# Start of a two-layer encoder trunk: products on the first 512 features, separate buffers for four w_ada blocks, another load order, and the rotary additions before the first maximum

## The chip, the cores and the metric

The kernel runs on one core of one Trainium2 chip. The metric is device time in microseconds (us) of one execution. The kernel before takes 1368.41 us, median of 3 runs (1368.14 to 1368.48).

## The reference

Two layers over 512 tokens of 1024 features, float32. In each layer (cut to what matters here):

```
c_act = silu(c)
mod = c_act @ w_ada[l] + b_ada[l]                 # 1024 -> 6144, six vectors of 1024
sh_a, sc_a, g_a, sh_m, sc_m, g_m = split(mod, 6)
h = x * (1 + sc_a) + sh_a
proj = h @ w_in[l]                                # 1024 -> 2208: a_q a_k a_v | b_cq b_ckv b_kr | c_q c_k c_v
y_a = dilated_mixture(a_q, a_k, a_v, rel_bias)    # 4 heads, bias per head from t5_bucket(key - query)
y_b = mla_attention(b_cq, b_ckv, b_kr, ...)       # 4 heads, 32 rotary features of 96
y_c = axial_gqa(c_q, c_k, c_v, ...)               # 8 query heads, 2 key heads
x = layer_norm(ALPHA * x + (1 + g_a) * (concat(y_a, y_b, y_c) @ w_o[l]))
h = x * (1 + sc_m) + sh_m
x = layer_norm(ALPHA * x + (1 + g_m) * (square(relu(h @ w1[l])) @ w2[l]))
```

## The kernel before

Each engine has its instructions written out in program order, and semaphores tie them together. Every float32 product is made of three fp32r products (`three`: high x high, high x low, low x high), so each weight slab (128 rows of a weight matrix, up to 512 columns) is loaded to `slab_raw`, copied to `slab_hi` by ScalarE (ACT) and subtracted to `slab_lo` by VectorE (DVE). These two are called the split of a slab. A ring of eight slab buffers is refilled by SyncE's queue (SP) in program order: slab i is issued only when slab i - 8 has been used, and all that stands behind it in the queue waits with it.

The first layer's start, which the change is about, goes so:

- `ada_load`, `ada_piece`: the vectors `mod` are made in blocks of 512 columns. A block of `w_ada` (2 MB) comes in two halves of 512 rows (1 MB each) into the two buffers `ada_w`; DVE adds up eight pieces per block (scalar times 128x512, plus the sum so far) in `ada_sum`, and TensorE (PE) adds over the partitions with a column of ones (`mod_cols`). A half may be loaded when the half two before it has been used. Blocks 0 and 1 are the shift `sh_a`, 2 and 3 the scale `sc_a`. All four are made first (`AHEAD = 4`).
- Between the blocks DVE and PE make one head's row of relative bias (`relb`, `onehot`, `lncnt`, `frow`: 128 equal rows of 1024), and ACT stores all of it in DRAM as `bias_rows` (2 MB). It is read back with a skew into `bands` during attention.
- Then x is transposed (`transpose_x`, tokens 0 to 255 as job `lnp`, 256 to 511 as `lnq`), scaled and shifted by ACT (`ln_evac`) and split in high and low (`hT_hi`, `hT_lo`, DVE: `ht_low`).
- `first_chunk` and `chunk_job` multiply it chunk by chunk with `w_in`: `cqa` (slabs 0 to 7), `cqkv` (8 to 15), `bcq` (16 to 23), `bckv` (24 to 31), `av` (32 to 39), then the transposes `tc` and `tk`, then `aqk` (40 to 47).
- Meanwhile DVE makes further modulation blocks, `ada(0, k)` behind the splits of slabs 8 to 15 and `ada(1, k)` behind those of 16 to 23, whose halves SP loads at the slabs named in `ADA_LOADS`, each when `ada_half` says that an earlier half has been used.
- ACT takes the finished `cqkv` out of PSUM only after the splits of slabs 16 to 21 and of `u_raw` (the weights `w_uq` and `w_ukv`); squares of it (`rsq`) go by DVE (`msq`) and GpSimd (POOL, `inv_sqrt`) to the rotary step `rope_tile` and to `c_roped`, on which PE's transposes `tc` wait.

Attention is a pipeline over 64 units of 128 queries: PE `score`, DVE maximum, ACT exponential, POOL normalisation, PE transposes, ACT and DVE split, PE product with v. In its first four steps DVE also does `rope_of_q(h)`, one addition of 32x512 each.

Of the kernel before, what the change touches and what calls it, by code (L numbers as in the profile page):

```python
# [27 lines left out]
S = 512  # L28
DEPTH = 2
P = 128  # L30
KT = D // P
# [21 lines left out]
AHEAD = 4  # L53


ADA_LOADS = {7: [0], 8: [1], 13: [2], 17: [3], 24: [4], 26: [5], 47: [6, 7], 55: [8, 9], 56: [10], 57: [11]}
# [71 lines left out]
def trunk(nc, t_in, out, scratch):  # L128
# [3 lines left out]
    with ExitStack() as ctx:  # L132
# [110 lines left out]
        relb = over("relb", [32, 4, P], 0)  # L243
        rel = over("rel", [32, 4], 2048)
        onehot = over("onehot", [32, 1024], 4096)
        lncnt = over("lncnt", [P, 1024], 8192)
        frow = over("frow", [P, 4, 1024], 12288)
# [32 lines left out]
        def sem(name):  # L280
# [3 lines left out]
        c_in, rel_in, table_in, const_in, x_in, small_in, up_in, ln_in, lnx_in, ropec_in = map(  # L284
            sem, ("c_in", "rel_in", "table_in", "const_in", "x_in", "small_in", "up_in", "ln_in", "lnx_in",
                  "ropec_in"))
        slab_in = [sem(f"slab_in{i}") for i in range(RING)]
        ada_in = [sem(f"ada_in{i}") for i in range(2)]
        band_in = [sem(f"band_in{i}") for i in range(2)]
        band_out, stored = sem("band_out"), sem("stored")  # L290
# [71 lines left out]
        def _(sp):  # L362
            sp.dma_start(c_col[:, 0, :], t_in["c_col"]).then_inc(c_in, 16)
            sp.dma_start(rel[:, :], t_in["rel_bias"]).then_inc(rel_in, 16)
# [8 lines left out]
            sp.wait_ge(setup_pool, 1)  # L373
            for n in range(2 * AHEAD):
                if n >= 2:
                    sp.wait_ge(ada_half, n - 1)
                ada_load(0, slice(512 * (n // 2), 512 * (n // 2) + 512), n % 2)
                if n == 1:
                    sp.dma_start(onehot[:, :], t_in["onehot"]).then_inc(table_in, 16)
                    sp.dma_start(lncnt[:, :], t_in["lncnt"].broadcast_to([P, 1024])).then_inc(table_in, 16)  # L380
                if n == 3:
                    sp.dma_start(X[:, :, :], t_in["x"].rearrange("(t p) d -> p t d", p=P)).then_inc(x_in, 16)
                if n == 2 * AHEAD - 1:
                    sp.dma_start(ropeT[:, :, :], t_in["ropeT"]).then_inc(const_in, 16)
                    sp.dma_start(ropeK[:, :, :, :], t_in["ropeK"]).then_inc(const_in, 16)
# [3 lines left out]

            for l in range(DEPTH):  # L390
                for i in range(PRE):
# [22 lines left out]
                    if l == 0 and i != 55:  # L414
                        ada_loads()
                    if i == 55:
# [7 lines left out]
                        for h in range(4):  # L424
                            if h >= 2:
                                wait_apart(sp, maxed, l * UNITS + 4 * (7 + h))
                            src = bass.AP(tensor=scratch.tensor, offset=scratch.offset + h * P * 1024 + 127,
# [80 lines left out]
        def _(pool):  # L508
# [11 lines left out]
            pool.wait_ge(setup_pool, 4)  # L520
            pool.affine_select(out=ident[:, :], in_=ones[:, :], compare_op=ALU.is_equal, fill=0.0, base=0,
                               pattern=[[-1, P]], channel_multiplier=1).then_inc(setup_pool, 1)
            pool.wait_ge(setup_pool, 5)
# [110 lines left out]
        def _(act):  # L634
# [3 lines left out]
            for b in range(AHEAD):  # L638
                act.wait_ge(mod_ready, b + 1)
                act.activation(mods[:, 4 * b:4 * b + 4], bank[b][:, 0:4], ACT.Copy,  # L640
                               bias=float(b >= 2)).then_inc(setup_act, 1)

            act.wait_ge(setup_dve, 2 + 4)
            act.dma_start(scratch.rearrange("h p n -> p h n"), frow[:, :, :]).then_inc(band_out, 16)
            act.wait_ge(x_in, 16)
            act.sem_inc(xhat_ready, TT)
            act.sem_inc(xhat_high, TT)

            for l in range(DEPTH):
# [56 lines left out]
                def slab_job_done(chunk):  # L706
                    act.wait_ge(slab_free, l * SLABS + RING + 8 * (chunk + 1))
# [13 lines left out]

                if l == 0:
                    norm_entry("lnp", 0, 0, 384)
                for k in range(8):
                    ln_evac("lnq", 0, k)
                for i in range(8, 16):
                    split(i, 384)
# [254 lines left out]
        def _(dve):  # L982
# [9 lines left out]
            SETUP_STEPS = 2 + AHEAD * 6  # L992

# [7 lines left out]
            dve.wait_ge(rel_in, 16)  # L1001
            dve.tensor_copy(relb[:, :, :], rel[:, :].unsqueeze(2).broadcast_to([32, 4, P])).then_inc(setup_dve, 1)
            for blk in range(AHEAD):
                for k in range(KT):
                    if k == 0:
                        dve.wait_ge(ada_in[0], (blk + 1) * 32)
                    elif k == 4:
                        dve.wait_ge(ada_in[1], (blk + 1) * 16)
                        dve.wait_ge(ada_half, 2 * blk + 1)
                    else:  # L1010
                        dve.wait_ge(dve_step, 2 + 6 * blk + k - k // 4)
                    ada_piece(k, blk).then_inc(ada_half if k % 4 == 3 else dve_step, 1)

                dve.wait_ge(table_in, 32)
                dve.wait_ge(setup_pe, blk + 1)
                dve.tensor_tensor(frow[:, blk, 0:512], bank[6][:, :], lncnt[:, 0:512], ALU.add)
                dve.tensor_tensor(frow[:, blk, 512:1024], bank[7][:, :], lncnt[:, 512:1024], ALU.add
                                  ).then_inc(setup_dve, 1)
            dve.wait_ge(setup_act, 1 + AHEAD)
            dve.tensor_copy(aff[:, 0, 0, :], mods[:, 8:16])  # L1020
            dve.tensor_copy(aff[:, 0, 1, :], mods[:, 0:8]).then_inc(aff_ready, 1)

            PER = DVE_STEPS
            for l in range(DEPTH):
# [29 lines left out]
                def ada(n, k):  # L1054
# [4 lines left out]
                    if k % 4 == 0:  # L1059
                        dve.wait_ge(ada_in[k // 4], (AHEAD + n + 1) * (32 if k == 0 else 16))  # L1060
# [10 lines left out]
                if l == 0:  # L1071
                    for k in range(4):
                        split(k, 384)
                    ht_low("lnp", 0)
                    for k in range(4):
                        ht_low("lnp", k + 1)
                        split(4 + k, 384)
                    for k in range(5, 8):
                        ht_low("lnp", k)
                for k in range(8):  # L1080
                    ht_low("lnq", k)
                for k in range(8):
                    split(8 + k, 384)
                    if l == 0:
                        ada(0, k)

# [142 lines left out]
                prepare_k(0)  # L1229
                for s in range(ATT_STEPS):  # L1230
# [16 lines left out]
                    if s < 4:  # L1247
                        rope_of_q(s)
# [165 lines left out]
                def ada_next(at, v):  # L1414

                    dve.wait_ge(mod_ready, at + (v - 1))
                    for k in range(KT):
                        if k % 4 == 0:
                            dve.wait_ge(ada_in[k // 4], (at + (v + 1)) * (16 if k else 32))
# [149 lines left out]
        def _(pe):  # L1569
            pe.sem_inc(slab_free, RING)  # L1570
            pe.wait_ge(setup_pool, 5)
# [390 lines left out]

DVE_STEPS = 260


def _tables():
# [72 lines left out]
```

## Time and profile before

| | |
|---|---|
| median of 3 runs | 1368.41 us |
| the profiled execution's own time | 1367.98 us |
| its span in the trace | 1366.1 us |
| PE busy | 1308.5 us, 96% |
| DVE busy | 983.9 us, 72% |
| ACT, POOL busy | 601.2 us, 318.7 us |
| PE busy in the first slices of 1/40 of the span (34 us) | 4 tenths in the first, 9 in the next ones |
| chain that ended last | PE 72%, DVE 13%, ACT 5%, DMA 4% |

The span is what the engines' records cover; the own time holds 1.9 us more around it. The page's second part shows PE at four tenths in its first slice and at nine tenths in nearly all others. Its chain follows the last instruction back to what released each step.

### The profile page before, as it was taken

Reading aid. Unit: us, or ns where it says so; the run is one execution under the profiler, and the core shown is the slowest. Engines: PE = TensorE matmul, PEld = TensorE weight load, DVE = VectorE, ACT = ScalarE, POOL = GpSimd, SP = SyncE. Lnnn points to the kernel's source line nnn. Section 1 sums busy time; section 2 is a strip of 40 time slices with the busy share of each in tenths; the row PEclk is TensorE's granted clock in tenths of the full one; section 3 lists DMA queues with packets and bytes.
Section 4 is the critical chain, followed back from the end, with each engine's and each line's share of the span. In section 5 each row is a group of like instructions: output and inputs, shape, how many; then the busy total and the mean of one; then the engine's idle time right before and its main releaser. Section 6 shows DMA issues by size and latency. Waiting matters only on the chain.

```text
span 1366.1 us, 19988 instructions
## 1 busy us (share of the span) xinstructions
PE 1308.5 (96%) x6888; PEld 1111.2 (81%) x6888; DVE 983.9 (72%) x1669; ACT 601.2 (44%) x1254; POOL 318.7 (23%) x427
## 2 busy tenths in 40 slices
PE   4999989999999999999999999999999999999996
PEld 2898878897978888888879977878898888888885
DVE  6668789976797678767764757998668565535677
ACT  0447589943532222223235657897163232222321
POOL 0004076631300110010020505776040100001005
PEclk9999999999999999999999999999999999999998
DMA  8765300223446545652224331010336222222222
GB/s 288 289 209 162 120 1 15 76 84 117 145 163 217 203 146 176 215 205 103 96 78 136 95 104 46 1 59 1 105 100 224 90 93 100 99 94 100 93 100 101
DMA packets 88454, 165.59 MB, mean 121 GB/s; under 512 B 8057, under 2 KB 18681, under 8 KB 88369
## 3 DMA queue, kind: packets, MB, share of 16 engines
q1 hardware_dynamic: 87696, 162.13, 34.6%
q10 hardware_dynamic: 672, 2.36, 0.5%
q8 instruction: 50, 0.82, 0.2%
q14 instruction: 36, 0.29, 0.1%
HBM read 160.26 MB, written 4.19 MB: 120 GB/s over the span
## 4 chain that ended last, share of the span: by engine, by line
PE 72%; DVE 13%; ACT 5%; DMA 4%; issue 3%; POOL 3%; SPq 0%; DVEq 0%; ACTq 0%; POOLq 0%
PE bank L1615 22%; PE bank L1617 22%; PE bank L1616 22%; PE bank L1846 3%; DVE ada_sum L997 3%; PE bank L1646 1%; DMA ada_b<-in_b_ada 1%; DMA slab_raw<-in_w 1%; DVE stats L1300 1%; PE bank L1576 1%; DVE sqr L1283 1%; ACT pt_hi L878 1%; POOL rms L546 1%; ACT k_hi L839 1%; ACT prob L867 1%
## 5 line engine op out<-in xcount | busy, mean ns | idle before, releaser
L1615 PE MATMUL bank<-hT_hi,slab_hi 128*128 128x512 f32 (+1 forms) x640 | 236.5, 370 | 3.8 <-DVE qC L1160 3.8
L1617 PE MATMUL bank<-hT_hi,slab_lo 128*128 128x512 f32 (+1 forms) x640 | 235.4, 368 | 0.0
L1616 PE MATMUL bank<-hT_lo,slab_hi 128*128 128x512 f32 (+1 forms) x640 | 235.4, 368 | 0.0
L1379 DVE TENSOR_TENSOR slab_lo<-slab_raw,slab_hi 128x512 fp32r<-128x512 f32 x240 | 166.6, 740 | 87.1 <-ACT slab_hi L939 64.4
L1615 PE MATMUL bank<-slab_hi,h_hi 128*128 128x512 f32 x512 | 200.5, 392 | 1.8 <-DVE slab_lo L1379 1.8
L1617 PE MATMUL bank<-slab_hi,h_lo 128*128 128x512 f32 x512 | 199.3, 389 | 0.0
L1616 PE MATMUL bank<-slab_lo,h_hi 128*128 128x512 f32 x512 | 199.2, 389 | 0.0
L1615 PE MATMUL bank<-slab_hi,hT_hi 128*128 128x384 f32 (+3 forms) x448 | 153.4, 342 | 4.7 <-issue 1.7
L1616 PE MATMUL bank<-slab_lo,hT_hi 128*128 128x384 f32 (+3 forms) x448 | 151.4, 338 | 0.0
L1617 PE MATMUL bank<-slab_hi,hT_lo 128*128 128x384 f32 (+3 forms) x448 | 151.4, 338 | 0.0
L1615 PEld LDWEIGHTS bank<-hT_hi,slab_hi 128*128 128x128 f32 x640 | 120.6, 188 | 26.2 <-DVE qC L1160 5.6
L1041 DVE TENSOR_TENSOR slab_lo<-slab_raw,slab_hi 128x512 fp32r<-128x512 f32 (+3 forms) x144 | 80.1, 585 | 79.1 <-ACT slab_hi L654 78.9
L1617 PEld LDWEIGHTS bank<-hT_hi,slab_lo 128*128 128x128 f32 x640 | 120.6, 188 | 20.1
L1616 PEld LDWEIGHTS bank<-hT_lo,slab_hi 128*128 128x128 f32 x640 | 120.7, 189 | 19.7
L997 DVE SCALAR_TENSOR_TENSOR ada_sum<-ada_w,c_col,ada_sum 128x512 f32<-128x512 f32 x168 | 128.0, 762 | 6.3 <-DMA ada_w<-in_w_ada 0.2
L654 ACT ACTIVATE slab_hi<-slab_raw 128x512 fp32r<-128x512 f32 (+3 forms) x144 | 74.7, 547 | 104.6 <-DMA slab_raw<-in_w_o 58.2
L1615 PEld LDWEIGHTS bank<-slab_hi,h_hi 128*128 128x128 f32 x512 | 96.1, 188 | 23.9 <-issue 4.1
L1617 PEld LDWEIGHTS bank<-slab_hi,h_lo 128*128 128x128 f32 x512 | 96.1, 188 | 20.2
L1616 PEld LDWEIGHTS bank<-slab_lo,h_hi 128*128 128x128 f32 x512 | 96.1, 188 | 19.9 <-issue 0.2
L1412 DVE TENSOR_TENSOR acc<-bank,acc 128x512 f32<-128x512 f32 x96 | 59.5, 681 | 63.0 <-PE bank L1617 63.0
L582 POOL TENSOR_TENSOR smax<-smax,mone 128x1 f32<-128x1 f32 x120 | 70.0, 583 | 137.9 <-ACT prob L867 137.7
L583 POOL TENSOR_SCALAR prob<-prob,smax 128x512 f32<-128x512 f32 x128 | 91.4, 714 | 21.7 <-DVE smax L1254 9.9
(207 smaller groups left out, 2441.9 us busy)
## 6 DMA issues: line engine op xcount, KB each, us to landing
slab_raw<-in_w SPq DMA_DIRECT2D x256, 256.0 KB, 2.7
ada_w<-in_w_ada SPq DMA_DIRECT2D x48, 1024.0 KB, 6.5
slab_raw<-in_w_in SPq DMA_DIRECT2D x48, 192.0 KB, 4.9
slab_raw<-in_w_o SPq DMA_DIRECT2D x32, 256.0 KB, 2.6
slab_raw<-in_w_in SPq DMA_DIRECT2D x16, 256.0 KB, 2.6
band<-bias_rows SPq DMA_DIRECT2D x8, 448.0 KB, 3.3
slab_raw<-in_w_in SPq DMA_DIRECT2D x16, 144.0 KB, 3.1
X<-in_x SPq DMA_DIRECT2D x1, 2048.0 KB, 9.5
```

What stands on the lines that cost most here:

```text
L546: pool.tensor_tensor(dst, dst, mhalf[:, 0:n], ALU.pow).then_inc(out_sem, 1)
L582: after(step(pool.tensor_tensor(smax[:, u % 4, 2:3], smax[:, u % 4, 1:2], mone[:, 0:1], ALU.pow)))
L583: pool.tensor_scalar(p, p, smax[:, u % 4, 2:3], 1.0, ALU.mult, ALU.mult).then_inc(normed, 1)
L654: act.activation(slab_hi[:, slot, 0:width], slab_raw[:, slot, 0:width], ACT.Copy).then_inc(slab_hi_done, 1)
L997: return dve.scalar_tensor_tensor(out=dst, in0=ada_w[:, k // 4, k % 4, :], scalar=c_col[:, 1, k:k + 1], in1=ada_b[:, :] if k == 0 else dst ...
L1041: dve.tensor_tensor(slab_lo[:, slot, 0:width], slab_raw[:, slot, 0:width], f32(slab_hi[:, slot, 0:width]), ALU.subtract).then_inc(slab_lo_ ...
L1379: dve.tensor_tensor(slab_lo[:, slot, :], slab_raw[:, slot, :], f32(slab_hi[:, slot, :]), ALU.subtract).then_inc(slab_lo_done, 1)
L1412: dve.tensor_tensor(dst, set_[t][:, :], dst, ALU.add).then_inc(evac_dve, 1)
L1615: pe.matmul(dst, a_hi, w_hi, start=first, stop=False)
L1616: pe.matmul(dst, a_hi, w_lo, start=False, stop=False)
L1617: return pe.matmul(dst, a_lo, w_hi, start=False, stop=last)
L1846: ins = pe.transpose(t_bank(u)[:, k * P:(k + 1) * P], prob[:, u % 4, k * P:(k + 1) * P], ident[:, :])
```

## The change

At the start of layer 0:

- The modulation is made in the order of `BOOT`: blocks 0 and 2 (shift and scale of features 0 to 511), then 1 and 3. Each of their eight halves has a buffer of its own, so no load waits for DVE. The biases of these blocks are added by DVE from a small tile (`boot_mods`), not through `ada_b`.
- SP issues two blocks first, then the small tables, slab 0, x in two parts, and then slabs and the other two blocks in turn. Slabs are numbered anew: 0 to 3 are `cqa` k 0 to 3, 4 to 7 `cqkv` k 0 to 3, 8 to 11 `cqa` k 4 to 7, 12 to 15 `cqkv` k 4 to 7.
- PE (`boot_chunks`) multiplies features 0 to 511 for `cqa` and for tokens 0 to 383 of `cqkv`, while DVE makes blocks 1 and 3. The transposed features 512 to 1023 wait in `xt_raw` until their scale is there. Tokens 384 to 511 of `cqkv` follow when the bank is free, and then k 4 to 7.
- The row of relative bias is one product of 33 rows with 4 columns for all heads (`lncnt` is its 33rd row), 16 KB are stored, and 16 copies of 128 KB from DRAM to DRAM make the 128 rows, one behind each slab load 24 to 39.
- `u_raw` is loaded at slab 19 (it was at 9), `ropeT` and `ropeK` at slab 20 (before the first slab until now). `ada(0, k)` comes in one piece after the splits of slabs 12 to 15, and the half that was loaded at slab 13 is loaded at slab 16.

In both layers `rope_of_q(0..3)` stands ahead of the first maximum.

```diff
+BOOT = [0, 2, 1, 3]
-ADA_LOADS = {7: [0], 8: [1], 13: [2], 17: [3], 24: [4], 26: [5], 47: [6, 7], 55: [8, 9], 56: [10], 57: [11]}
+ADA_LOADS = {16: [2], 17: [3], 24: [4], 26: [5], 47: [6, 7], 55: [8, 9], 56: [10], 57: [11]}
...
         @block.sync
+            for n in range(4):
+                boot_load(n)
+            sp.dma_start(rel[0:32, :], t_in["rel_bias"]).then_inc(rel_in, 16)
+            sp.dma_start(onehot[:, :], t_in["onehot"]).then_inc(table_in, 16)
+            sp.dma_start(boot_bias[:, :], t_in["b_first"]).then_inc(bias_in, 16)
+            boot_slabs(C_QA, range(1))
+            x_load(0)
+            x_load(1)
+            boot_slabs(C_QA, range(1, 4))
+            boot_load(4)
+            boot_load(5)
+            boot_slabs(C_QKV, range(4))
+            boot_load(6)
+            boot_load(7)
+            boot_slabs(C_QA, range(4, 8))
...
+            sp.wait_ge(mod_ready, 1)
+            for n in range(2):
+                ada_load(0, slice(512 * ADA_COLS[0], 512 * ADA_COLS[0] + 512), n)
+            boot_slabs(C_QKV, range(4, 8))
...
+                    if l == 0 and 24 <= i < 40:
+                        h, part = divmod(i - 24, 4)
+                        if i == 24:
+                            sp.wait_ge(band_out, 16)
+                        sp.dma_start(scratch[h, 32 * part:32 * part + 32, :],
+                                     scratch[h, P:P + 1, :].broadcast_to([32, 1024])).then_inc(band_wide, 16)
-                    if i == 9:
+                    if i == (9 if l else 19):
...
         @block.scalar
+                    for k in range(4):
+                        act.wait_ge(bank_ready, 2 * (k + 1))
+                        boot_hT(k)
+                        if k < 3:
+                            split(k + 1, 384)
+                    boot_raw(4)
+                    boot_raw(5)
+                    for n in range(4, 8):
+                        split(n, 384)
+                    boot_raw(6)
+                    boot_raw(7)
+                    for n in range(8, 12):
+                        split(n, 384)
+                    act.wait_ge(evac_act, 12)
+                    act.wait_ge(aff_ready, 1)
+                    for k in range(4, 8):
+                        boot_hT(k)
+                    for n in range(12, 16):
+                        split(n, 384)
...
         @block.tensor
+                    product("cqa", 0, 0)
+                    product("cqa", 1, 1)
+                    turn_high(4)
+                    turn_high(5)
+                    product("cqa", 2, 2)
+                    turn_high(6)
+                    turn_high(7)
+                    product("cqa", 3, 3)
+                    for k in range(3):
+                        product("cqkv", k, 4 + k, range(3))
+                    pe.wait_ge(evac_act, 12)
+                    pe.wait_ge(ada_half, 6)
+                    mod_cols(turned[3], ada_sum[:, 2, :], 0)
+                    product("cqkv", 3, 7, range(3))
+                    pe.wait_ge(ada_half, 8)
+                    mod_cols(turned[3], ada_sum[:, 3, :], 4)
+                    pe.wait_ge(aff_ready, 1)
+                    for k in range(4):
+                        product("cqkv", k, 4 + k, range(3, 4))
+                    for k in range(4, 8):
+                        product("cqa", k, 4 + k)
+                    for k in range(4, 8):
+                        product("cqkv", k, 8 + k)
...
         @block.vector
                 prepare_k(0)
+                for h in range(4):
+                    rope_of_q(h)
                 for s in range(ATT_STEPS):
...
-                    if s < 4:
-                        rope_of_q(s)
```

How the order changes on DVE from the program's start, before:

```order
L990 TENSOR_TENSOR c_col<-c_col 128x8
L1002 COPY relb<-rel 32x512
L997 SCALAR_TENSOR_TENSOR ada_sum<-ada_w,c_col,ada_b 128x512
L997 SCALAR_TENSOR_TENSOR ada_sum<-ada_w,c_col,ada_sum 128x512 x7
L1016 TENSOR_TENSOR frow<-bank,lncnt 128x512
L1017 TENSOR_TENSOR frow<-bank,lncnt 128x512
```

and after:

```order
L1079 TENSOR_TENSOR c_col<-c_col 128x8
L1109 TENSOR_SCALAR ada_sum<-ada_w,c_col 128x512
L1111 SCALAR_TENSOR_TENSOR ada_sum<-ada_w,c_col,ada_sum 128x512 x7
L1109 TENSOR_SCALAR ada_sum<-boot_w,c_col 128x512
L1111 SCALAR_TENSOR_TENSOR ada_sum<-boot_w,c_col,ada_sum 128x512 x7
L1092 TENSOR_TENSOR slab_lo<-slab_raw,slab_hi 128x384
L1123 TENSOR_TENSOR aff<-bank,boot_bias 128x4
L1124 SCALAR_TENSOR_TENSOR aff<-bank,boot_bias 128x4
L1131 TENSOR_TENSOR hT_lo<-tmp,hT_hi 128x512
```

Scale and shift (`aff`) of four of the eight feature tiles follow on two blocks instead of four, and the additions into `frow` are gone.

How the order changes in SP's queue around slabs 16 to 21 (`u_raw`, `ropeT`, `ropeK` are the loads that moved), before:

```order
L369 DMA ada_w<-in_w_ada 128x4x512
L388 DMA slab_raw<-in_w_in 128x384 x6
L388 DMA slab_raw<-in_w_in 128x288
```

and after:

```order
L377 DMA ada_w<-in_w_ada 128x4x512
L383 DMA slab_raw<-in_w_in 128x384 x2
L448 DMA u_raw<-in_w_uq 128x3x512
L450 DMA u_raw<-in_w_ukv 128x2x512
L383 DMA slab_raw<-in_w_in 128x384
L439 DMA ropeT<-in_ropeT 128x1024
L440 DMA ropeK<-in_ropeK 128x256
L383 DMA slab_raw<-in_w_in 128x384 x3
```

Behind the `w_ada` half that is issued at slab 17, slabs 18 and 19 come first as before, but 1920 KB of other loads now lie between slab 19 and slab 21.

## Rows read from the trace of the kernel before

**Rows 1.** Stretches: busy us (count) per engine, granted clock, DMA share, GB/s

```profile
0.00:48.00 48.00, 25.77 (x65) 15.30 (x66) 32.92 (x54) 5.69 (x15) 1.23 (x9) 1.00 0.85 307
48.00:100.00 52.00, 51.26 (x294) 50.45 (x294) 29.95 (x62) 28.29 (x65) 0.00 (x0) 1.00 0.64 224
...
10.00:20.00 10.00, 8.39 (x16) 4.10 (x16) 7.33 (x11) 0.17 (x1) 0.00 (x0) 1.00 0.94 340
...
84.00:88.00 4.00, 4.00 (x25) 4.00 (x24) 1.69 (x3) 0.48 (x1) 0.00 (x0) 1.00 1.05 393
```

**Rows 2.** Timeline of the start: start us, us, engine, line, op, [idle before it <- releaser]

```profile
1.72 0.42 SPq L369 DMA_DIRECT2D ada_w<-in_w_ada  x1
...
6.86 0.75 DVE L997 SCALAR_TENSOR_TENSOR ada_sum<-ada_w,c_col,ada_b 128x512 f32<-128x512 f32 x1 [3.05 <-DMA ada_b<-in_b_ada]
7.64 5.54 DVE L997 SCALAR_TENSOR_TENSOR ada_sum<-ada_w,c_col,ada_sum 128x512 f32<-128x512 f32 x7
...
23.04 1.87 PE L1576 MATMUL bank<-ones,ada_sum 128*128 128x1 f32 x8 [2.19 <-DVE ada_sum L997]
...
44.48 3.65 PE L1646 MATMUL bank<-ident,X 128*128 128x128 f32 x16 [0.65 <-ACTq L646]
```

**Rows 3.** Timeline of PE: two neighbours early, two neighbours 2 us later

```profile
49.53 0.52 PE L1617 MATMUL bank<-slab_hi,hT_lo 128*128 128x384 f32 x1
...
49.85 0.39 PE L1615 MATMUL bank<-slab_hi,hT_hi 128*128 128x384 f32 x1
...
51.99 0.33 PE L1615 MATMUL bank<-slab_hi,hT_hi 128*128 128x384 f32 x1
...
52.17 0.33 PE L1616 MATMUL bank<-slab_lo,hT_hi 128*128 128x384 f32 x1
```

**Rows 4.** Timelines of DVE, SP, ACT and PE, 80 to 98 us

```profile
80.75 0.55 DVE L1041 TENSOR_TENSOR slab_lo<-slab_raw,slab_hi 128x384 fp32r<-128x384 f32 x1
81.22 0.75 DVE L997 SCALAR_TENSOR_TENSOR ada_sum<-ada_w,c_col,ada_sum 128x512 f32<-128x512 f32 x1
...
82.41 4.77 SPq L388 DMA_DIRECT2D slab_raw<-in_w_in  x7
...
87.52 2.13 ACT L654 ACTIVATE slab_hi<-slab_raw 128x384 fp32r<-128x384 f32 x4 [4.93 <-DMA slab_raw<-in_w_in]
89.55 2.70 ACT L738 ACTIVATE u_hi<-u_raw 128x512 fp32r<-128x512 f32 x5
...
97.81 0.41 PE L1615 MATMUL bank<-slab_hi,hT_hi 128*128 128x384 f32 x1 [0.44 <-ACT slab_hi L654]
```

**Rows 5.** Timelines of DVE, ACT and PE, 99 to 137 us

```profile
99.37 2.99 DVE L1128 TENSOR_REDUCE msq<-rsq 128x10 f32<-128x640 f32 x4
...
136.19 1.84 ACT L804 ACTIVATE cqT_hi<-bank,colpack 128x512 fp32r<-128x512 f32 x3
...
136.42 0.50 PE L1615 MATMUL bank<-hT_hi,slab_hi 128*128 128x512 f32 x1 [0.48 <-DVE qC L1160]
```

**Rows 6.** Timelines of DVE, POOL and PE where attention starts, last row layer 1

```profile
172.07 0.69 DVE L1245 TENSOR_REDUCE smax<-bank 128x1 f32<-128x512 f32 x1 [3.35 <-PE bank L1823]
172.79 0.68 DVE L1200 TENSOR_TENSOR qB<-tmp 32x512 f32<-32x512 f32 x1
...
173.73 0.54 POOL L582 TENSOR_TENSOR smax<-smax,mone 128x1 f32<-128x1 f32 x1 [49.73 <-ACT prob L867]
...
179.08 0.69 POOL L583 TENSOR_SCALAR prob<-prob,smax 128x512 f32<-128x512 f32 x1
...
180.50 0.69 DVE L1260 TENSOR_TENSOR pt_lo<-bank,pt_hi 128x512 fp32r<-128x512 f32 x1
...
181.25 0.33 PE L1615 MATMUL bank<-pt_hi,v_hi 128*64 128x256 f32 x1 [0.57 <-DVE pt_lo L1260]
...
840.92 0.33 PE L1615 MATMUL bank<-pt_hi,v_hi 128*64 128x256 f32 x1 [0.70 <-DVE pt_lo L1260]
```

**Rows 7.** DMA issues up to 230 us: engine, op, count, KB each, us to landing

```profile
bias_rows<-frow ACTq DMA_DIRECT2D x1, 2048.0 KB, 8.3
```

More of the change, by code:

```diff
@@ L720, in mods_evac, with boot_hT @@
                     evac(mods[:, 24:32], src[:, 8:16], bias=1.0)
-                if l == 0:
[L723 to L727, printed above, removed]
+                def boot_hT(k):
+                    src = banks(JOB["lnp"])[k][:, :] if k < 4 else xt_raw[:, k - 4, :]
+                    move = dict(scale=aff[:, 0, 0, k:k + 1], bias=aff[:, 0, 1, k:k + 1])
+                    if k >= 2:
+                        act.wait_ge(ht_ready, 2 * (k - 1))
+                    ins = act.activation(tmp[:, k % 2, :], src, ACT.Identity, **move)
+                    if k < 4:
+                        ins.then_inc(evac_act, 1)
+                    act.activation(hT_hi[:, k, :], src, ACT.Identity, **move).then_inc(evac_act, 1)
@@ L728, in _ @@
+                if l == 0:
+                    boot()
+                else:
+                    for k in range(8):
+                        ln_evac("lnq", 0, k)
+                    for i in range(8, 16):
+                        split(i, 384)
                 for k in range(6):
@@ new lines, in boot_low @@
+            def boot_low(k):
+                dve.wait_ge(evac_act, 2 * k + 2 if k < 4 else 9 + k)
+                dve.tensor_tensor(hT_lo[:, k, :], tmp[:, k % 2, :], f32(hT_hi[:, k, :]), ALU.subtract
+                                  ).then_inc(ht_ready, 2)
+            for b in range(2):
+                for k in range(KT):
+                    boot_piece(b, k)
+            boot_split(0)
+            dve.wait_ge(bias_in, 16)
+            boot_mods(0, bank[4][:, 0:4], bank[5][:, 0:4], boot_aff)
@@ new lines, in _ @@
+            boot_low(0)
+            boot_split(1)
+            boot_low(1)
+            boot_split(2)
+            boot_piece(2, 0)
+            boot_low(2)
+            boot_split(3)
+            boot_piece(2, 1)
+            boot_low(3)
+            for k in range(2, 4):
+                boot_piece(2, k)
+            for k in range(4):
+                boot_split(4 + k)
+                boot_piece(2, 4 + k)
+            for k in range(8):
+                boot_piece(3, k)
+            boot_split(8)
@@ L1023, in _ @@
+            boot_split(9)
+            late = banks(JOB["lnp"])[3]
+            boot_mods(1, late[:, 0:4], late[:, 4:8], aff_ready)
+            boot_split(10)
+            boot_low(4)
+            boot_split(11)
+            for k in range(5, 8):
+                boot_low(k)
+            for n in range(12, 16):
+                boot_split(n)
+            SETUP_STEPS = setup_steps[0]
             PER = DVE_STEPS
@@ L1071, in _ @@
                 if l == 0:
[L1072 to L1084, printed above, removed]
-                        ada(0, k)
+                    for k in range(8):
+                        ada(0, k)
+                else:
+                    for k in range(8):
+                        ht_low("lnq", k)
+                    for k in range(8):
+                        split(8 + k, 384)
                 dve.wait_ge(small_in, l * 32 + 32)
```

215 lines of the change are left out of this document (140 added, 75 removed).

## The prediction

> **What bounds the kernel now.** I first cut the span into stretches. Up to 48 us PE is busy for 25.8 us only, and the next 52 us it is busy for 51.3 [rows 1]. So the first 48 us are a stage in which PE waits, and afterwards it hardly ever does. The timeline of the start says for what: the first `w_ada` half is issued at 1.72, DVE starts on it at 6.86 and needs 0.78 us a piece (5.54 for seven, one behind the other) [rows 2], 6.2 us a block. Four blocks come one after another, with loads that wait for DVE's buffers, and only then does PE transpose x, at 44.48, for 3.65 us [rows 2]. The first product runs at 48.1. DMA moves 340 GB/s from 10 to 20 us and 393 from 84 to 88 [rows 1]; DVE is busy 33 of 48 us. The start is bound by loads and DVE together.
>
> From 48 us on PE looks saturated, but the chain of waits runs elsewhere, and this decides what an earlier start is worth. DVE ends the last piece of `ada(0)` at 81.97 (81.22 + 0.75). SP, held until then, issues a `w_ada` half and slabs 18 to 24 at 82.41. ACT sits 4.93 us for slab 18, splits four slabs, does `u_hi` at 89.55, and PE waits 0.44 for slab 22 at 97.81 [rows 4]. Then msq on DVE at 99.37, POOL's powers, the rotary tiles, and at 136.42 PE waits for DVE's `qC` before `aqk` [rows 5]. From there to the first maximum at 172.07 PE works through. The 38.6 us from 97.81 to 136.42 are fixed work in a fixed order on DVE, ACT and POOL, which the change leaves alone. So the gain is the time by which slab 22 is ready earlier.
>
> **Part 1: first product.** Ahead of all of x SP now issues four halves (4.2 MB), small tables and slab 0 (0.34 MB), then 2.1 MB of x. The first half was issued at 1.72 and used at 6.86 behind the row `ada_b`; now it goes 0.5 us sooner: 6.3. At 340 GB/s a half takes 3.1 us: 6.3, 9.4, 12.5, 15.6. DVE's four pieces of a half take 3.1 too and end at 18.7. x is complete at 15.6 + 7.2 = 22.8, its first half at 19.7. PE transposes tokens 0 to 255 (8 at 0.23, from 3.65 / 16 [rows 2]) to 21.5 and does `mod_cols` for 1.87 [rows 2], to 23.4. DVE's two small additions: 23.9. ACT's two passes over 128x512 at 0.61 each (1.84 for three [rows 5]): 25.2. DVE's subtraction 0.69 [rows 6]: **first product at 26**, 22 us sooner than 48.1.
>
> **Part 2: the second scale and shift.** DVE still owes, from 23.9: 16 pieces at 0.78 (12.5), nine slab splits at 0.55 [rows 4] (5.0) and four low parts (2.8), 20.3 together. I add 2.5 for two waits on ACT (its first pass of 1.2 us, and slab 4, which it splits only behind PE's transposes and two copies), and 0.5 for `mod_cols` and `boot_mods`: scale and shift ready at **47.2**. Loads keep up: blocks 1 and 3 with slabs 1 to 7 are 5.6 MB behind x, 16 us, to 39. The removed additions into `frow` and the narrower store cost nothing here. PE has, up to there, four slabs of `cqa` (2.08 each: 12 products at 0.173 apart, which the two neighbours at 51.99 and 52.17 show to rounding [rows 3]), eight transposes twice, three and one slabs of 36 products (1.56 each) and `mod_cols`: 18 to 20 us from 26. It fits just under DVE.
>
> After 47.2 PE does tokens 384 to 511 (2.1) and eight slabs (16.6), to 66. DVE: low parts behind ACT (4 x 1.22), then slabs 12 to 15, which SP can only issue from 47.7 on when PE frees them, split by 55.1; then `ada(0)`, 6.2 us: **61.3**. The same point was 81.97: 20.7 us sooner. I take 0.1 off for `cqa`'s evacuation, which stands behind slab 17.
>
> **Part 3: what is given back.** SP sits on `ada_half` at slabs 16 and 17 as it did, and then issues everything at once. Before slab 21 now come `u_raw`, `ropeT` and `ropeK`, 1920 KB more, which were loaded in quieter times. At 393 GB/s that is 5.0 us, at 340 it is 5.8; I take 5.4. So ACT gets to `u_hi` at about 74.1 where it was 89.55, and slab 22 at 82.6 where it was 97.81: **15.2 us** is what arrives at `aqk`. PE on its own would have wanted slab 22 at 66 + 6 x 2.08 = 78.5, so it now waits there for some 4 us, a wait ten times that of before [rows 4].
>
> **Part 4: the 16 copies.** Each is 128 KB between slab loads 24 to 39. The trace shows no copy inside DRAM. Nearest below: at the 340 GB/s of loads, 0.39 us. Nearest above: the store of the same rows, 2048 KB in 8.3 us beside other loads [rows 7], 0.52 each, and twice that if reading and writing don't overlap, 1.04. At 0.39 the 16 need 6 us in a stretch of some 25 us of `bckv` and `av`, hidden in the ring's lead. At 1.04 slabs come each 1.45 us and slab 37 is 2 us late for ACT's order. I take 0.2, nearer the lower end, since each row of a copy is 4 KB in one piece, where a slab's is 1 to 1.2 KB; the range keeps 0 to 2.5. From a page alone: the Trainium skill (DMA: Bandwidth & Descriptors, Latency and other measured facts) gives about 214 GB/s for copies between DRAM tensors; an estimate from it is 0.6 us each, still hidden.
>
> **Part 5: rotary additions.** DVE idles 3.35 us before the first maximum and each addition takes 0.68 [rows 6]; four, 2.8, fit in. In the fill they lay between the first maxima, on the chain. With them gone POOL is next: it starts at 173.73, and ends unit 3 at 179.77 (179.08 + 0.69) [rows 6], four units back to back. PE's transposes of unit 3 follow, and the first product with v, now at 181.25 behind `pt_lo` at 180.50 and 0.57 of waiting [rows 6], can move by no less than this 0.57 and by 1.4 if POOL's passes shrink to 0.69 with DVE quiet. I take **1.0 per layer**, 2.0 in all; layer 1 starts in the same way (840.92, wait 0.70 [rows 6]). A loss has no place to come from: the additions end before the maximum could start.
>
> **Sum.** 15.2 - 0.2 + 2.0 = 17.0 us. From the profiled execution's 1367.98 (span 1366.1 and 1.9 around it): 1350.98. The median is 0.43 above the profiled one: **1351.4 us**.
>
> **Rivals.**
>
> *PE-bound after all (0.13).* If slab 21 comes by 70, because the loads interleave or DVE's start is quicker, PE's own work sets the pace: 97.37 (97.81 less its wait) - 78.5 = 18.9, with the fill 20.9 less: 1347. For it: DMA reached 393 GB/s. Against: ACT must pass `u_hi`, the evacuation and the squares before slab 22, some 7 us from 89.55 to the split ahead of 97.81 [rows 4].
>
> *PE at its lower level (0.11).* Neighbouring products of 384 columns stand 0.32 us apart at 49.53 and 49.85, and 0.18 apart at 51.99 and 52.17 [rows 3]: 384 / 0.32 is 1.2 GHz, the other is the 2.4 level, though the row of granted clock reads 1.00 for 48 to 100 us [rows 1]. PE had been mostly waiting before. Now its first products are fed by ACT and DVE at about 2 us a slab, with gaps. If half of the 20 us of this part run at 0.32 instead of 0.17, the second scale is not late but `cqa` and `cqkv` are, by 8: 1360. The Trainium skill (TensorE: Matmul & The Clock Gate, HAM oscillation) warns of just this, bursts with waits between them that fall back to the half clock each time; by it the sum would be the 1360. Against: a slow PE has no gaps, as DVE's 2 us a slab feed it faster than the 3.8 it then needs.
>
> *The copies hold the ring (0.06 that they cost 3 or more, 0.02 of it slower than before).* This is the case of the other sign. It has one mechanism: each copy T us long on all engines of DMA; eleven stand ahead of slab 37, so ACT's order slips by 11 x (T - 1.04) + 2. It eats the 17 us at T = 2.4, that is 55 GB/s, and beyond that the kernel is slower, 1370 and up. At T = 1.5 it would be 1358. Nothing in the trace is that slow.
>
> *The change does not do it (0.04).* If x or the first halves come so late that DVE's idle time only moves, `ada(0)` still ends near 82: then only the fill is left, 1366, or nothing. Against: DVE's wait for loads between blocks is visible and its buffers are no longer shared.
>
> **How the numbers follow.** Forecast 0.66: its own range is 1348.5 to 1356.5 (load rate 0.8, DVE waits 2, copies 2.3, fill 0.8 either way). The range of eight in ten takes in the PE-bound case and most of the lower-level one: **1346 to 1359**. A measurement of this kernel can tell about 0.2% from no change, 2.7 us. Faster by more 0.94, within it 0.04, slower 0.02.
>
> **What would show it.** First `hT` product near 26 and the last scale near 47; the last piece of `ada(0)` near 61; `u_hi` near 74; PE waiting some 4 us for slab 22 in `bcq`, at 82 to 83; `aqk` behind `qC` near 121; first maximum near 157, no DVE addition between the first four maxima, and POOL back to back. The forecast fails if DVE reaches the second `boot_mods` much later than 47, if the copies' landings exceed 1 us each beyond the queue ahead of them, or if products of 384 columns stay 0.32 apart beyond 30 us.

## The result, and the profile after

The changed kernel takes 1349.78 us, median of 4 runs (1349.47 to 1350.61), against 1368.45 for the kernel before (1368.14 to 1369.84): a ratio of 0.9862, with a 95% interval of 0.985 to 0.9875. The prediction was 1351.4 in a range of 1346 to 1359. The profiled execution took 1349.8 us with a span of 1348.1, which is 18.0 less than the 1366.1 of before. The sum of the prediction was 17.0. One of the eleven executions of run 1 below, 1875 us at a granted clock of 0.66, is a slow one; without it the median of run 1 would be 1365.28 and not 1365.36.

The windows of the changed kernel answer to [rows 1]. The columns are the window, its length, busy time and count of PE, PEld, DVE, ACT and POOL, then granted clock, DMA share and GB/s.

```profile
0.00:48.00 48.00, 33.07 (x167) 29.04 (x168) 32.30 (x56) 18.32 (x33) 1.33 (x10) 1.00 0.90 329
48.00:100.00 52.00, 48.49 (x287) 47.99 (x286) 35.74 (x69) 27.75 (x68) 14.65 (x16) 0.93 0.69 240
10.00:20.00 10.00, 6.61 (x18) 3.42 (x19) 8.68 (x13) 1.59 (x3) 0.00 (x0) 1.00 1.04 405
```

In the first 48 us PE is busy for 33.1 us where it was 25.8, and in them it now does products. DMA moves 405 GB/s from 10 to 20 us, where it moved 340. The next window is no longer full, and its granted clock has dropped to 0.93.

The timelines of DVE, PE, ACT and SP in the changed kernel, at the places that the prediction named, answer to [rows 2, 3, 4]:

```profile
6.59 0.48 DVE L1109 TENSOR_SCALAR ada_sum<-ada_w,c_col 128x512 f32<-128x512 f32 x1 [3.05 <-DMA ada_w<-in_w_ada]
7.12 5.54 DVE L1111 SCALAR_TENSOR_TENSOR ada_sum<-ada_w,c_col,ada_sum 128x512 f32<-128x512 f32 x7
...
25.17 0.66 PE L1769 MATMUL bank<-slab_hi,hT_hi 128*128 128x384 f32 x1 [1.17 <-issue]
...
44.92 0.15 DVE L1124 SCALAR_TENSOR_TENSOR aff<-bank,boot_bias 128x4 f32<-128x4 f32 x1
...
54.29 5.55 DVE L1084 SCALAR_TENSOR_TENSOR ada_sum<-ada_w,c_col,ada_sum 128x512 f32<-128x512 f32 x7
...
61.31 0.48 SPq L448 DMA_DIRECT2D u_raw<-in_w_uq  x1
...
72.35 2.70 ACT L827 ACTIVATE u_hi<-u_raw 128x512 fp32r<-128x512 f32 x5
...
80.60 0.66 PE L1769 MATMUL bank<-slab_hi,hT_hi 128*128 128x384 f32 x1 [3.50 <-ACT slab_hi L692]
```

The first product stands at 25.2 (before: 47.8). The second scale is done at 45.1. `ada(0)` ends at 59.8, 22.1 us earlier than before; `u_hi` starts at 72.4 and slab 22 comes at 80.6, both 17.2 earlier. So 4.9 us are given back between the end of `ada(0)` and `u_hi`, and SP's issue of `u_raw` ahead of slab 21 stands right there. PE waits 3.50 us for slab 22.

The wait has something behind it that the prediction did not have. Windows of PE alone (window, length, busy, granted clock, DMA share, GB/s) around it:

```profile
60.00:66.00 6.00, 6.00 (x35) 1.00 1.05 389
78.00:80.00 2.00, 0.00 (x0) 0.83 0.00 0
80.00:82.00 2.00, 1.40 (x4) 0.50 0.04 8
82.00:84.00 2.00, 2.00 (x8) 0.50 0.35 28
84.00:86.00 2.00, 2.00 (x8) 0.50 0.95 352
86.00:88.00 2.00, 2.00 (x14) 0.96 1.07 405
```

Behind the wait the granted clock is 0.50, the level of 1.2 GHz, until about 86 us. In a window of 2 us PE does 8 products where it otherwise does some 12 (35 in 6 us above). The wave of work behind slab 22 was 17.2 us early at its start, and the last product of `av` ends 16.1 us early. This 1.1 us is lost on PE alone. The next product of PE that waits for `qC` stands at 132.19 in the kernel before, behind a wait of 0.87, and at 114.99 here, without one: 17.2 early again. So the slow clock delayed PE where others had to be waited for anyway.

Where attention starts, the timelines of DVE, POOL and PE in the changed kernel answer to [rows 6]:

```profile
151.67 2.77 DVE L1339 TENSOR_TENSOR qB<-tmp 32x512 f32<-32x512 f32 x4
155.10 1.89 DVE L1386 TENSOR_REDUCE smax<-bank 128x1 f32<-128x512 f32 x3 [0.66 <-PE bank L2024]
...
157.41 0.70 POOL L632 TENSOR_SCALAR prob<-prob,smax 128x512 f32<-128x512 f32 x1
...
161.34 0.70 POOL L632 TENSOR_SCALAR prob<-prob,smax 128x512 f32<-128x512 f32 x1
...
162.50 0.36 PE L1769 MATMUL bank<-pt_hi,v_hi 128*64 128x256 f32 x1
...
820.73 0.36 PE L1769 MATMUL bank<-pt_hi,v_hi 128*64 128x256 f32 x1
```

The first maximum is 16.97 us early (172.07 - 155.10) and the first product with v 18.75 (181.25 - 162.50): the fill itself gained 1.78. In layer 1 the product with v is 20.19 early (840.92 - 820.73). The span ends 18.0 early. So something between 820 us and the end takes 2.2 us back.

### The profile page after: what moved, and what is told of

Its sections match the earlier page's. It is cut to its first block, busy times and chain, and to the rows that moved or that the text cites. A ratio compares the mean times of both kernels' runs of the same rounds, so it can differ in the third digit from the quotient of the medians.

```text
span 1348.1 us, 19960 instructions
## 1 busy us (share of the span) xinstructions
PE 1297.1 (96%) x6876; PEld 1106.5 (82%) x6876; DVE 974.4 (72%) x1646; ACT 604.3 (45%) x1248; POOL 317.8 (24%) x428
## 4 chain that ended last, share of the span: by engine, by line
PE 76%; DVE 11%; ACT 5%; issue 3%; DMA 3%; POOL 2%; SPq 0%; DVEq 0%; ACTq 0%
PE bank L1769 23%; PE bank L1770 23%; PE bank L1771 23%; PE bank L2047 3%; DVE ada_sum L1084 1%; PE bank L1715 1%; DVE h_lo L1526 1%; DVE sqr L1524 1%; DMA slab_raw<-in_w 1%; DVE stats L1439 1%; DVE sqr L1422 1%; ACT k_hi L928 1%; ACT prob L956 1%; ACT pt_hi L967 1%; DMA onehot<-in_onehot 1%
## 5 line engine op out<-in xcount | busy, mean ns | idle before, releaser
L1187 DVE TENSOR_TENSOR slab_lo<-slab_raw,slab_hi 128x512 fp32r<-128x512 f32 (+3 forms) x128 | 71.5, 590 | 72.5 <-ACT slab_hi L692 72.4
L1084 DVE SCALAR_TENSOR_TENSOR ada_sum<-ada_w,c_col,ada_sum 128x512 f32<-128x512 f32 x140 | 107.0, 765 | 7.1 <-DMA ada_w<-in_w_ada 1.9
L1769 PEld LDWEIGHTS bank<-slab_hi,hT_hi 128*128 128x128 f32 x448 | 85.7, 191 | 16.0 <-issue 3.9
```

Source lines behind the costliest of these rows:

```text
L1084: return dve.scalar_tensor_tensor(out=dst, in0=ada_w[:, k // 4, k % 4, :], scalar=c_col[:, 1, k:k + 1], in1=ada_b[:, :] if k == 0 else dst ...
L1187: dve.tensor_tensor(slab_lo[:, slot, 0:width], slab_raw[:, slot, 0:width], f32(slab_hi[:, slot, 0:width]), ALU.subtract).then_inc(slab_lo_ ...
L1769: pe.matmul(dst, a_hi, w_hi, start=first, stop=False)
```

## The experiments

Each kernel was timed in up to five rounds beside the kernel before on its own chip. The medians of that kernel there were 1368.56 (early weights, rotary, doubled copies), 1368.96 (pieces first, two buffers) and 1368.77 (the last three). Single executions of a changed kernel differed by 2 to 4 us and those of the kernel before by up to 6, so the medians tell about 1 us apart, and for less I go by the rows.

**1. The rotary additions alone.** The kernel before, with this edit only:

```diff
                 prepare_k(0)
+                for h in range(4):
+                    rope_of_q(h)
                 for s in range(ATT_STEPS):
...
-                    if s < 4:
-                        rope_of_q(s)
```

> The kernel before, with the rotary additions moved ahead of the first maximum and nothing else. My theory after the result: the fill of the attention pipeline is set by DVE's additions between the maxima, and then by POOL, whose passes take 0.70 us instead of up to 1.08 when DVE leaves it alone, so each layer gains 1.6 to 1.8 us and the kernel 2 to 3.3 (about 1365 to 1366.5). The prediction's own term was 1.0 a layer, 2.0 in all. The rival, that the fill's gain in the changed kernel belongs to the earlier start and its TensorE clock and not to this edit, gives under 0.7 us in all here. What I look for: POOL's first four powers back to back, the first product with v 7.4 us behind the first maximum instead of 9.2, and the granted clock of the fill (0.5 to 0.66 before) at 1.00 or not.

Measured: 1365.36 us, ratio 0.9978 (0.9968 to 0.9987), 3.2 us faster. Timelines of POOL and PE of this kernel:

```profile
172.78 0.54 POOL L582 TENSOR_TENSOR smax<-smax,mone 128x1 f32<-128x1 f32 x1 [49.74 <-ACT prob L867]
173.43 0.70 POOL L583 TENSOR_SCALAR prob<-prob,smax 128x512 f32<-128x512 f32 x1
...
177.35 0.70 POOL L583 TENSOR_SCALAR prob<-prob,smax 128x512 f32<-128x512 f32 x1
...
178.52 0.36 PE L1615 MATMUL bank<-pt_hi,v_hi 128*64 128x256 f32 x1
...
836.91 0.36 PE L1615 MATMUL bank<-pt_hi,v_hi 128*64 128x256 f32 x1
```

POOL's fourth pass starts 4.57 us behind its first minimum (177.35 - 172.78), where it was 5.35 [rows 6]. From the first maximum to the first product with v it is 7.4 us in both layers (171.12 and 829.52 are the maxima), where it was 9.18 and 9.17. The edit is worth 1.78 a layer without any of the other parts. The granted clock from 174 to 182 us is 1.00, and this leaves a rival: in the kernel before it was 0.56 and 0.58 from 176 to 180 us, so the gain could be PE's clock. Run 2 settles this.

**2. The rotary additions put back.** The same edit reversed in the changed kernel.

> The changed kernel with the rotary additions back between the first four maxima. If the edit's gain is its own, 1.5 to 3.3 us slower than the changed kernel, 1351.3 to 1353; if the changed kernel's gain in the fill came with the earlier start, within 0.7 us of it, about 1350.

Measured: 1353.41 us (1352.21 to 1354.34); the changed kernel had 1349.78 and, in its later repetition, 1350.26. That is 3.2 to 3.6 slower. The timeline of POOL and PE in it:

```profile
157.44 1.08 POOL L632 TENSOR_SCALAR prob<-prob,smax 128x512 f32<-128x512 f32 x1
...
159.14 0.81 POOL L632 TENSOR_SCALAR prob<-prob,smax 128x512 f32<-128x512 f32 x1
...
162.15 0.70 POOL L632 TENSOR_SCALAR prob<-prob,smax 128x512 f32<-128x512 f32 x1
...
164.32 0.34 PE L1769 MATMUL bank<-pt_hi,v_hi 128*64 128x256 f32 x1 [0.70 <-DVE pt_lo L1399]
```

POOL's passes of the same shape take 1.08 and 0.81 again while DVE adds between the maxima, and the wait for `pt_lo` is back. In layer 0 the granted clock falls again too (0.50 from 159 to 161 us). In layer 1 it does not, and so this fill shows the additions without the slow clock. DVE and PE there, then windows of PE:

```profile
815.40 0.69 DVE L1384 TENSOR_REDUCE smax<-bank 128x1 f32<-128x512 f32 x1 [3.35 <-PE bank L2024]
...
824.59 0.33 PE L1769 MATMUL bank<-pt_hi,v_hi 128*64 128x256 f32 x1 [0.71 <-DVE pt_lo L1399]
```

```profile
819.00:821.00 2.00, 1.75 (x12) 1.00 0.00 0
821.00:823.00 2.00, 1.50 (x8) 1.00 0.00 0
```

From the first maximum to the first product with v it takes 9.19 us at the full clock (824.59 - 815.40) and 9.18 in layer 0 at the half (164.32 - 155.14). So the fill's gain is not PE's clock. A part of the gain, about 0.6 us (0.38 and twice 0.11), is POOL's own speed when DVE does not add beside it; the fourth minimum, 0.71 here and 0.55 in the changed kernel, adds 0.16. The Trainium skill (GPSIMD Engine Reference, Specifications) says that GpSimd shares its SBUF interfaces with VectorE and names instructions with two SBUF inputs as a source of contention; the additions, whose inputs lie in SBUF, are of this kind, and the rows agree.

**3. Early weights.** The changed kernel, with the loads of the three tiles issued behind slab 15, where SP would otherwise wait, and taken out at slabs 19 and 20:

```diff
             boot_slabs(C_QKV, range(4, 8))
+            sp.dma_start(u_raw[:, 0:3, :], t_in["w_uq"][0].rearrange("(k p) n -> p k n", p=P)).then_inc(up_in, 16)
+            sp.dma_start(u_raw[:, 3:5, :], t_in["w_ukv"][0].rearrange("(k p) n -> p k n", p=P)).then_inc(up_in, 16)
+            sp.dma_start(ropeT[:, :, :], t_in["ropeT"]).then_inc(const_in, 16)
+            sp.dma_start(ropeK[:, :, :, :], t_in["ropeK"]).then_inc(const_in, 16)
...
-                    if i == (9 if l else 19):
+                    if l and i == 9:
```

> The changed kernel with u_raw, ropeT and ropeK issued behind slab 15 and ahead of slab 16, so while SP would otherwise stand waiting, and no longer ahead of slab 21. The theory that the 1920 KB between them and slab 21 set the time of slab 22: ACT does u_hi at about 68 us instead of 72.4, slab 22 is split by about 75.5, PE wants it at about 77.1, its wait of 3.5 us goes and with it the stretch at half clock from 80 to 86; the kernel gains 3.5 to 4.6 us, to about 1345.5. The rival that another wait takes its place (slab 16 and 17 behind the tables, ada_w, ACT's order, or powers on POOL) gives under 1 us.

Measured: 1344.25 us (1342.98 to 1346.49), ratio 0.9824 (0.981 to 0.9837): 5.5 to 6 us faster than the changed kernel, and 24 faster than the kernel before. The timelines of DVE and ACT, and a window over all engines, in this kernel:

```profile
54.96 5.54 DVE L1085 SCALAR_TENSOR_TENSOR ada_sum<-ada_w,c_col,ada_sum 128x512 f32<-128x512 f32 x7
...
68.01 2.70 ACT L828 ACTIVATE u_hi<-u_raw 128x512 fp32r<-128x512 f32 x5
...
76.00:80.00 4.00, 4.00 (x25) 4.00 (x24) 4.00 (x7) 0.94 (x3) 1.09 (x2) 1.00 0.23 34
80.00:84.00 4.00, 4.00 (x29) 4.00 (x28) 2.01 (x6) 0.44 (x1) 3.83 (x3) 1.00 1.05 380
```

From the end of `ada(0)` (60.50) to `u_hi` it is 7.5 us, as in the kernel before (89.55 - 81.97 = 7.6), against 12.5 in the changed kernel. PE has no wait at slab 22 and the granted clock stays 1.00. The profiled execution ends 4.3 us before the changed kernel's (spans 1343.8 and 1348.1), and the rows account for this much; the medians, taken on different chips, differ by a little more. The theory holds. The rival of another wait holds for a small rest. The loads ahead of slab 16 make `ada(0)` end 0.66 later (60.50 and 59.84), so of the 5.0 won behind it 4.34 are there at `u_hi`, and of these 3.93 at the first maximum (155.10 - 151.17).

**4. Copies twice.** Every copy of a bias row is issued a second time, into four more heads of `bias_rows` that nothing reads, and the wait for the copies is doubled:

```diff
                         sp.dma_start(scratch[h, 32 * part:32 * part + 32, :],
                                      scratch[h, P:P + 1, :].broadcast_to([32, 1024])).then_inc(band_wide, 16)
+                        sp.dma_start(scratch[h + 4, 32 * part:32 * part + 32, :],
+                                     scratch[h, P:P + 1, :].broadcast_to([32, 1024])).then_inc(band_wide, 16)
```

> The changed kernel with each of the 16 copies issued twice, the second time into rows that nothing reads, and the wait for them doubled. If the copies are hidden in the ring's lead, as the trace has it, within 0.7 us of the changed kernel. If they hold the ring, and were paid in the changed kernel, by 0.4 to 1 us each: 4 to 10 us slower.

Measured: 1353.35 us (1352.52 to 1355.26), some 3.3 slower. This is between the two expectations, below the 4 to 10 of the second. The list of waits of this kernel from 95 to 116 us (engine and line waited for, total, times, longest):

```profile
ACT slab_hi L694 <- DMA slab_raw<-in_w_in: 3.1, 4, 1.5
PEld bank L1771 <- issue: 2.3, 1, 2.3
PE bank L1771 <- DVE slab_lo L1189: 2.1, 1, 2.1
```

None of the three stands in the same stretch of the changed kernel. Sixteen further copies put the slabs late, and the first product with v from 162.50 to 167.35. Of these 4.85 us the span shows 2.7; in layer 1 they are still 4.6, and the rest goes by the clock of layer 1, which is treated below. It does not say what the first sixteen cost: the lead may have been just enough, or already short. That needed the mirror of it, run 8.

**5. All pieces first.** DVE multiplies all four blocks before it makes the first scale; loads, buffers and PE's order stay:

```diff
-            for b in range(2):
+            for b in range(4):
                 for k in range(KT):
                     boot_piece(b, k)
             boot_split(0)
...
-            boot_piece(2, 0)
...
-            for k in range(8):
-                boot_piece(3, k)
```

> The changed kernel with DVE multiplying all four blocks of w_ada before the first scale and shift are made, as the kernel before did, so that no product begins on 512 features; loads, buffers and PE's order stay. DVE ends its 32 pieces when the last half has landed, 36 to 39 us, and the first product stands at about 41 instead of 25.2. PE then has all its work at once and needs 49.3 us from the first product to slab 22, as before: 90, against 80.6. So 8 to 12 us slower than the changed kernel, 1358 to 1362: the early start is worth that, and own buffers and load order the other 7 or so. The rival, that the time of slab 22 is a matter of SP's late loads alone and the first product's time is not on the path, gives under 2 us.

Measured: 1365.08 us (1364.03 to 1366.57), 15 slower, more than I expected. Timelines of DVE and PE in this kernel:

```profile
37.98 0.15 DVE L1124 SCALAR_TENSOR_TENSOR aff<-bank,boot_bias 128x4 f32<-128x4 f32 x1
...
40.51 0.66 PE L1762 MATMUL bank<-slab_hi,hT_hi 128*128 128x384 f32 x1 [16.63 <-DVE hT_lo L1131]
...
60.79 0.16 DVE L1123 TENSOR_TENSOR aff<-bank,boot_bias 128x4 f32<-128x4 f32 x1 [7.89 <-PE bank L1708]
...
96.76 0.66 PE L1762 MATMUL bank<-slab_hi,hT_hi 128*128 128x384 f32 x1 [3.86 <-ACT slab_hi L692]
```

The first product came where I had put it, 15.3 us later than in the changed kernel (40.51 - 25.17). My mistake was behind it: I took the 49.3 us to slab 22 from the kernel before, but PE's order was left as in the changed kernel, with the second `mod_cols` only behind seven slabs, and there the stretch takes 56.3 (55.4 in the changed kernel). The second scale at 60.9 waits for PE 7.89 us. So the whole 15.3 and 0.9 more are there at slab 22 (96.76 - 80.60), and by the medians 14.8 to 15.3 reach the end. This run says that the start on 512 features is worth about 15 us in this order of PE, and it is no fair trial of a kernel without halving, which would order PE otherwise.

**6. Two buffers.** The own buffers stay, but SP waits as if there were two:

```diff
                 blk = BOOT[n // 2]
+                if n >= 2:
+                    sp.wait_ge(ada_half, n - 1)
```

> The changed kernel, whose w_ada halves from the third on wait until DVE has used the half two before, as with two shared buffers; order and memory stay. SP stands still while DVE multiplies, and x and the slabs behind it start later: the first product 2 to 4 us later, the second scale as much. 2 to 5 us slower if own buffers matter; the rival, that DVE's work fills this time anyway (the slack is PE's), gives under 1 us.

Measured: 1357.09 us (1356.25 to 1358.02), 7.3 slower than the changed kernel's first median, more than the 2 to 5. SP and DVE in this kernel:

```profile
1.24 0.97 SPq L392 DMA_DIRECT2D ada_w<-in_w_ada  x2
9.52 3.58 SPq L392 DMA_DIRECT2D boot_w<-in_w_ada  x2
...
51.77 0.16 DVE L1125 TENSOR_TENSOR aff<-bank,boot_bias 128x4 f32<-128x4 f32 x1 [0.41 <-PE bank L1717]
```

The queue issues nothing from 2.2 to 9.5 us. The first product is 3.6 late (28.77), and the further halves, behind waits of their own, add as much again: the second scale is 6.9 late and slab 22 8.3 (88.85). I had counted the delay once; it comes at each pair of halves.

**7. The changed kernel again**, on the chip of the next two.

> The changed kernel itself, so that the others have it on their own chip: 1349.8, and no more than 1 us from it.

Measured: 1350.26 us (1348.78 to 1350.77).

**8. Copies later.** The 16 copies behind slabs 38 to 53, where DMA is idle for long stretches:

```diff
-                    if l == 0 and 24 <= i < 40:
-                        h, part = divmod(i - 24, 4)
-                        if i == 24:
+                    if l == 0 and 38 <= i < 54:
+                        h, part = divmod(i - 38, 4)
+                        if i == 38:
```

> The changed kernel with its 16 copies issued behind slabs 38 to 53 in place of 24 to 39. Doubling the copies made aqk 4.85 us later, with ACT waiting seven times for slabs, so the single copies had used up the ring's lead and may already have a price. If they have, aqk comes 0.3 to 1.5 us earlier than in the changed kernel (116.3) and the kernel gains as much; if the lead covered them fully, as I predicted (0.2), the time is the same within 0.5 us.

Measured: 1349.75 us (1348.52 to 1350.72), 0.5 from the repetition, inside the scatter. The first product with v stands at 162.58 against 162.50 and 162.46. With the copies out of the way nothing comes earlier there, so the single copies were covered entirely. Run 4 shows that twice as many are not.

**9. Early weights and late copies.** Runs 3 and 8 together.

> Early weights and late copies together: u_raw, ropeT and ropeK ahead of slab 16, and the copies behind slabs 38 to 53. With the wait for slab 22 gone, bckv and av ask for slabs faster, and in the run with early weights alone only 3.7 of the 4.3 us at u_hi arrived at aqk. If the copies took the missing 0.6, this kernel is 0.5 to 1.5 us faster than that one, about 1343.3; if not, 1344.2 again.

Measured: 1344.74 us (1343.84 to 1345.74), the same as run 3 within the scatter. The first product with v is 0.3 us earlier (158.23 and 158.55), and this doesn't reach the end. The copies are not the next limit there either.

## Why the prediction was right, and where its steps were off

**First product: 26 predicted, 25.2 measured.** Most of it is the loads, which ran at 405 GB/s and not 340: PE transposes the first half of x from 18.7 and not from 19.7. DVE's part came out as forecast, 18.6 for 18.7, by two misses that cancel: the first piece of a block takes 0.48 us and not 0.78, since `TENSOR_SCALAR` takes the place of the addition of a bias row, but DVE began at 6.6 and not at 6.3. ACT's two passes took 1.45 us and not 1.22. The "48.1" for the first product before was read wrong by 0.3; it stands at 47.78, and the sum does not use it.

**Second scale: 47.2 predicted, 45.1 measured; `ada(0)` ends at 59.8 and not 61.3.** Of these 2.1 us, 1.4 were there at the first scale (22.5 and not 23.9). The 2.5 that I had put down for two waits of DVE on ACT were an allowance without a row, and too small: the waits are four and take 3.8 (1.84, 0.59, 0.19, 1.18). The work was put too large, at 20.3, and DVE is busy for 18.0, since neighbours on DVE overlap (a split of 0.55 is followed after 0.47, a low part of 0.69 after 0.61). The two misses mostly cancel, and 1.5 are left at the end of `ada(0)`, most of what the forecast missed at slab 22.

**Given back by u_raw, ropeT and ropeK: 5.4 predicted, 4.9 measured.** Run 3 shows the cause. The products behind it agree: the fourth that waits for `qC` stands at 119.5 (forecast 121), and the first maximum at 155.1 (157). The shift at slab 22 was therefore 17.2 and not the 15.2 of the sum: 1.5 from the start and 0.5 from here. The wait of PE was put at 4 us and is 3.50, for the slab that was named.

**Copies: 0.2 predicted, 0 measured** (run 8). From issue to landing a copy of 128 KB took 3.3 us in the median, but copies and slabs are under way at the same time. Run 4 puts the price of sixteen more at 3.3 us in the median and at 4.85 at the first product with v, 0.3 each by that row. This is less than the 0.39 of my lower bound, and part of it may lie in the lead still; it is no measurement of a copy alone.

**Rotary additions: 1.0 a layer predicted, 1.78 measured** (run 1: 1.78 and 1.77). This term was mis-sized most, and in its bounds too, which ended at 1.4. The step that failed was to take the wait of 0.57 for all that DVE holds up, and a value between this alone and this with POOL's faster passes, where the two add. The rows split the 1.78. POOL's fourth pass starts 0.78 sooner behind its first minimum (4.57 for 5.35). From this pass to the first product with v it then takes 1.16 us (162.50 - 161.34) and not 2.17 (181.25 - 179.08), 1.01 sooner, and only 0.57 of this showed as a wait of PE. In the kernel before DVE works without a gap from 172.07 to 180.37, so DVE sets the fill there; in the changed kernel it has gaps, and PE waits for POOL instead.

**What took the excess back.** At slab 22 the shift was 2.0 more than forecast and the fills gave 3.55 and not 2.0. Had all that arrived, the span would be 20.8 us shorter (17.2 + 3.55). It is 18.0 shorter. So that the total came so near the forecast is in part luck: terms that were 3.8 too small together met a loss of 2.8 that was not foreseen. The slow clock behind slab 22 is not this loss, since its 1.1 us were made good by `qC`; 0.2 were gone at the first maximum. The larger loss is in layer 1. PE of the kernel before, and then of the changed kernel, around the same pause, 13 us behind the first product with v of layer 1:

```profile
852.00:854.00 2.00, 1.92 (x15) 1.00 0.01 4
854.00:856.00 2.00, 0.02 (x1) 1.00 0.00 0
856.00:858.00 2.00, 2.00 (x16) 1.00 0.00 0
```

```profile
832.00:834.00 2.00, 1.76 (x14) 1.00 0.00 0
834.00:836.00 2.00, 0.19 (x2) 1.00 0.00 0
836.00:838.00 2.00, 2.00 (x13) 0.77 0.00 0
838.00:840.00 2.00, 2.00 (x10) 0.50 0.04 8
840.00:842.00 2.00, 2.00 (x15) 0.88 0.00 0
```

PE is idle for 2 us in both. Behind it the clock falls to 0.50 in the one and stays in the other. The profiled executions of all kernels fall into two groups by this. From the product with v of layer 1 to the end of the span it takes 527.2 to 527.5 us where the clock falls (the changed kernel, its repetition, runs 3, 5, 8 and 9) and 525.2 to 525.9 where it does not (before, runs 1, 2, 4 and 6). The means of the groups are 1.8 us apart, and the windows of the changed kernel, at 0.77, 0.50 and 0.88 for 2 us each, lose 1.7 us of full clock, so the fall costs some 1.8. Of the missing 2.8 us this is the largest part; the last 0.8, spread over both layers, I did not trace to a cause. Which kernels have it was not settled: the pause is the same, and no change here touches that place. One execution of each was profiled, so it isn't known either whether a kernel has it always. The mean granted clock of the changed kernel's own four executions is 0.993 twice and 0.995 twice, which speaks against always.

**The rivals.** PE as the bound after all did not happen in the changed kernel, since slab 21 was not there by 70; run 3, which takes the loads away, is that case, and its 1344.25 lies below the 1347 that I gave for it, by the fills and the loads together. PE at its lower level happened at the start for only nine products, 0.32 us apart from 25.6 to 27.9, and 0.17 after that. The Trainium skill's rule (TensorE: Matmul & The Clock Gate, HAM oscillation) had no long waits to act on in the stretch that I tried it on, where PE was busy for 21.1 of the 22.5 us from the first scale to the second, but it describes the wait for slab 22, where I had not applied it: behind 3.50 us without a product the granted clock was 0.50. The copies did not hold the ring. The narrower bias rows (one product for all heads, a store of 16 KB) were not tried alone, and no run shows what they are worth.

## What to carry to other kernels

When a start is shortened, list every load that used to run in its idle time, and issue those in the queue's new idle time, ahead of its next wait: here 1.9 MB left ahead of one slab cost 4.9 of 22.1 us, and issuing them earlier brought 4.3 back at the end of the span. Work moved off a chain between engines can be worth the wait that shows and also what the neighbour engine gains when it runs alone, so look whether these terms add. A wait of PE shows less than the engine behind it holds up when PE has other delayed work to fill the time. A new wait of PE can be followed by the half clock; whether this costs anything is read at the next point where PE waits for another engine (here nothing).

## What the runs showed of the hardware

- A wait of 3.5 us on PE was followed by some 5 us at granted clock 0.50. The pause of 2 us in layer 1 was followed by a fall in six profiled executions and by none in five.
- POOL's pass over 128x512 takes 0.70 us alone and 0.81 to 1.08 beside DVE's additions (runs 1 and 2).
- Loads into SBUF ran at 405 GB/s over 10 us, and 389 over 6 us, on this one core.
- DVE multiplies 128x512 by a column in 0.48 us, and multiplies and adds in 0.74 to 0.79.
- The granted clock read 1.00 at 25 to 28 us, while neighbouring products of 384 columns stood 0.32 us apart, twice their distance from 28.3 us on. For the first products, spacing is the better witness.
